# Expert weights in a mixture-of-experts tail: three interleaved runs of blocks, and gathers by row whose indices can be out of bounds

## The reference

```
    padded = (counts + MOE_BLOCK - 1) // MOE_BLOCK * MOE_BLOCK
    ...
    def expert_block(args):
        rows, e = args
        xb = t_pad[rows]
        hid = jax.nn.silu(xb @ w_gate[e]) * (xb @ w_up[e])
        return hid @ w_down[e]
    ...
    y = jnp.zeros((N + 1, D), jnp.float32).at[row_tok].add(y_rows)[:N]
```

## Time and profile before

| | before |
|---|---|
| median of 3 runs | 3672.84 us (3671.2 to 3678.9) |
| the profiled execution | 3669.79 us |
| its span in the trace | 3667.9 us |
| mean granted TensorE clock | 0.981 |
| PE busy, share of the span | 94% |
| DMA issues of expert weights | 48 of 3072.0 KB, 11.8 us to landing (median) |

### The profile page before, as it was taken

One profiled execution on the slowest core, in us unless ns is written; L12 is line 12 of the kernel. 1 busy time (PEld: TensorE's weight loads), 2 busy tenths in 40 slices (PEclk: granted clock), 3 DMA queues, 4 the chain that ended last, 5 costly groups with the idle time before them and its releaser, 6 DMA issues. The chain is left out here.

```text
span 3667.9 us, 32753 instructions
## 1 busy us (share of the span) xinstructions
PE 3460.3 (94%) x11181; PEld 1792.6 (49%) x11181; DVE 1707.4 (47%) x4073; ACT 1046.7 (29%) x2551; POOL 1000.7 (27%) x1395
## 2 busy tenths in 40 slices
PE   4999899999999999999999998899999986999998
PEld 3754355555444644444444444555664433444443
DVE  4656633343355484326655556644454553222222
ACT  3122122221110362002234446643332221222221
POOL 0277767500000393000000002655651001222221
PEclk8999999999999999999999999999999998999999
DMA  3133444433245112222221000000102215999997
GB/s 140 57 131 138 145 157 155 140 126 109 97 160 176 64 36 81 107 88 92 81 85 35 23 9 12 1 1 1 69 25 104 98 75 214 325 336 337 330 331 237
DMA packets 115562, 451.55 MB, mean 123 GB/s; under 512 B 15635, under 2 KB 43155, under 8 KB 103356
## 3 DMA queue, kind: packets, MB, share of 16 engines
q1 hardware_dynamic: 91484, 370.18, 28.3%
q0 software_dynamic: 18432, 58.74, 6.0%
q10 hardware_dynamic: 5472, 20.45, 1.5%
HBM read 340.28 MB, written 117.42 MB: 125 GB/s over the span
## 5 line engine op out<-in xcount | busy, mean ns | idle before, releaser
L142 PE MATMUL pst<-arena 128*128 128x512 f32 (+4 forms) x6554 | 2694.8, 568 | 48.5 <-DMA arena<-in_w_exp 25.5
L142 PEld LDWEIGHTS pst<-arena 128*128 128x128 f32 x6554 | 1243.9, 196 | 1337.6 <-issue 1232.4
L164 POOL TENSOR_TENSOR arena<-arena 128x4 f32<-128x4 f32 (+7 forms) x784 | 403.3, 514 | 455.7 <-DVE arena L2060 395.3
L164 DVE TENSOR_TENSOR arena<-arena 128x1 f32<-128x1 f32 (+8 forms) x1260 | 460.1, 366 | 95.0 <-ACT arena L2290 20.1
L147 PE MATMUL pst<-arena 128*128 128x128 f32 x2161 | 328.1, 286 | 100.3 <-DVE arena L246 52.5
L147 PEld LDWEIGHTS pst<-arena 128*128 128x128 f32 x2161 | 260.7, 146 | 278.5 <-issue 153.2
L1286 POOL TENSOR_SCALAR arena<-arena 128x384 f32<-128x384 f32 (+1 forms) x128 | 151.7, 1213 | 555.8 <-DVE arena L1278 554.6
L153 ACT ACTIVATE arena<-pst,arena 128x128 f32<-128x128 f32 (+1 forms) x630 | 244.8, 485 | 92.7 <-PE pst L147 90.2
L2237 POOL TENSOR_SCALAR arena<-arena 128x512 f32<-128x512 f32 (+3 forms) x160 | 218.6, 1390 | 150.5 <-DVE arena L164 137.2
L167 DVE TENSOR_SCALAR arena<-arena 128x1 f32<-128x1 f32 (+11 forms) x581 | 141.2, 243 | 194.9 <-DMA arena<-in_bc 80.0
L152 ACT ACTIVATE arena<-pst 128x512 f32<-128x512 f32 (+4 forms) x250 | 124.7, 518 | 323.9 <-PE pst L142 197.1
(11 more groups left out here) (200 smaller groups left out, 2070.4 us busy)
## 6 DMA issues: line engine op xcount, KB each, us to landing
arena<-in_w_exp SPq DMA_DIRECT2D x48, 3072.0 KB, 11.8
arena<-in_w_ada SPq DMA_DIRECT2D x48, 512.0 KB, 4.8
rotd<-arena POOLq DMA_DIRECT2D x32, 512.0 KB, 4.0
arena<-rotd SPq DMA_DIRECT2D x32, 512.0 KB, 4.7
arena<-sgd SPq DMA_DIRECT2D x16, 1024.0 KB, 7.1
arena<-pwd SPq DMA_DIRECT2D x32, 416.0 KB, 5.6
pwd<-arena SPq DMA_DIRECT2D x16, 576.0 KB, 6.1
h2d<-arena SPq DMA_DIRECT2D x17, 512.0 KB, 2.9
```

Source lines behind the costliest of these rows:

```text
L142: x = t.do.matmul(o, l, r, start=(i == 0), stop=(i == len(pairs) - 1))
L164: own(v, s).tensor_tensor(o, a, b, op).then_inc(*inc(s, *event))
```

## The change

The order of blocks changes. Program block b no longer stands for place b of the sorted list but for place `sB[b]`: 0, 16, 32, 1, 17, 33, 2, 18, 34 and so on to 15, 31, 47 (48 to 62 stay). So weights slot b % 3 sees one third of the sorted list in order. For program blocks 0 to 47 the experts then are 0 15 22, 1 16 23, 2 17 24, 3 18 25, 4 18 25, 5 18 26, 5 19 26, 6 19 27, 7 19 28, 8 20 28, 9 20 29, 10 21 29, 11 21 30, 12 22 30, 13 22 31, 14 22 31.

The weights of the first three blocks come through SP in two transfers each (`w_up`, 16 KB in each partition, and `w_down`, 8 KB). All later ones come through POOL as gathers by row, again in two parts. The index of partition p is 128 times the expert plus p; where the expert is that of the block three before, 65536 p is added, which puts every row but partition 0's out of bounds, and such rows are not fetched (`oob_is_err=False`). The `up` part waits for `up` of three blocks before, the `down` part for `down` of three blocks before. The row gather is issued one block earlier than it was. The index table `wI` takes a few more operations on DVE, POOL and PE.

```
@@ te_rt, ve_rt
-            trs(t, [(bank(6)[0:1, 0:128], bcol[:, 1:2])]).then_inc(*inc("rt_pe", "bE"))
+            t.do.matmul(bank(6)[:, 0:64], ones, dg, start=True, stop=True).then_inc(*inc("rt_pe", "bE"))
...
-            ts(v, q, bcol[:, 1:2], bcol[:, 1:2], 31.0, None, MIN, BYP, "owner")
+            ts(v, q, bcol[:, 1:2], bcol[:, 1:2], 31.0, None, MIN, BYP)
+            ts(v, q, dg, sB, bcol[:, 2:3], bcol[:, 1:2], ALU.is_equal, MUL, "owner")
             own(v, q).tensor_copy(nbI, pen[:, 31:32]).then_inc(*inc(q, "nb"))
             v.wait_ge(*at("rt_pe", "bE"))
             v.do.tensor_copy(bE[0:1, :], bank(6)[0:1, 0:64]).then_inc(*inc(q, "bE"))
+            ts(v, q, wf, bank(6)[:, 0:64], 128.0, bcol[:, 2:3], MUL, ADD)
+            tt(v, q, same[:, 3:64], wf[:, 3:64], wf[:, 0:61], ALU.is_equal)
+            stt(v, q, same[:, 3:64], same[:, 3:64], bcol[:, 3:4], wf[:, 3:64], MUL, ADD)
+            own(v, q).tensor_copy(wI[:, 3:64], same[:, 3:64]).then_inc(*inc(q, "wI"))
...
@@ the loads
-        def sp_moe_load(s, b):
+        def sp_moe_first(s):
             for i in range(2):
                 s.wait_ge(*at(f"st_out{i}", "x3", NT - 2 + i))
             s.wait_ge(*at("rt_ve", "bE"))
-            s.wait_ge(*at("moe_pe", "down", b - 3, 1))
-            e = s.do.value_load(bE[0:1, b:b + 1], min_val=0, max_val=31)
-            s.do.dma_start(WX[b % 3], T["w_exp"][bass.ds(e, 1), :, :].rearrange("a p n -> p (a n)")
-                           ).then_inc(*dma(f"moe_wx{b % 3}", "wx", b))
+            for b in range(3):
+                e = s.do.value_load(bE[0:1, b:b + 1], min_val=0, max_val=31)
+                s.do.dma_start(WX[b][:, 0:4096], T["w_up"][bass.ds(e, 1), :, :].rearrange("a p n -> p (a n)")
+                               ).then_inc(*dma(f"moe_wf{b}", "up", b))
+                s.do.dma_start(WX[b][:, 4096:6144], T["w_down"][bass.ds(e, 1), :, :].rearrange("a p n -> p (a n)")
+                               ).then_inc(*dma(f"moe_wf{b}", "down", b))
+
+        def po_moe_load(p, b, part):
+            p.wait_ge(*at("rt_ve", "wI"))
+            for i in range(3):
+                p.wait_ge(*at(f"moe_wf{i}", "down", i))
+            if part == "up":
+                p.wait_ge(*at("moe_pe", "up", b - 3))
+                o, w = WX[b % 3][:, 0:4096], T["w_up"]
+            else:
+                p.wait_ge(*at("moe_pe", "down", b - 3, 1))
+                o, w = WX[b % 3][:, 4096:6144], T["w_down"]
+            p.do.indirect_dma_start(out=o, out_offset=None, in_=w.rearrange("a p n -> (a p) n"),
+                                    in_offset=bass.IndirectOffsetOnAxis(ap=wI[:, b:b + 1], axis=0),
+                                    bounds_check=4095, oob_is_err=False
+                                    ).then_inc(*dma(f"moe_{part}{b % 3}", "w", b))
...
@@ POOL's run
-            for b in range(lo, min(lo + 2, hi)):
+            for b in range(lo, min(lo + 3, hi)):
+                if b >= 3:
+                    po_moe_load(p, b, "up")
+                    po_moe_load(p, b, "down")
                 po_moe_gather(p, b)
             for b in range(lo, hi + 1):
-                if b + 2 < hi:
-                    po_moe_gather(p, b + 2)
+                if b + 3 < hi:
+                    po_moe_gather(p, b + 3)
+                    po_moe_load(p, b + 3, "up")
                 if b > lo:
+                    if lo + 3 <= b + 2 < hi:
+                        po_moe_load(p, b + 2, "down")
                     po_moe_scatter(p, b - 1)
```

More of the change, by code:

```diff
@@ L2662, in build @@
         idf = reg(115.5, 64)
+        sB, wf, same, dg = (reg(115.75 + 0.25 * i, 64) for i in range(4))
+        wI = reg(116.75, 64).bitcast(U32)
         bE = reg(117, 64).bitcast(I32)
@@ L2683, in po_rt @@
                       ).then_inc(*inc("rt_po"))
+            p.do.iota(bcol[:, 2:3], [[0, 1]], base=0, channel_multiplier=1, allow_small_or_imprecise_dtypes=True
+                      ).then_inc(*inc("rt_po"))
+            p.do.iota(bcol[:, 3:4], [[0, 1]], base=0, channel_multiplier=65536, allow_small_or_imprecise_dtypes=True
+                      ).then_inc(*inc("rt_po"))
+            p.do.iota(sB[:, 0:48].rearrange("p (a b) -> p a b", a=16), [[1, 16], [16, 3]], base=0, channel_multiplier=0,
+                      allow_small_or_imprecise_dtypes=True).then_inc(*inc("rt_po"))
+            p.do.iota(sB[:, 48:64], [[1, 16]], base=48, channel_multiplier=0, allow_small_or_imprecise_dtypes=True
+                      ).then_inc(*inc("rt_po"))
             p.do.memset(LT, 0.0).then_inc(*inc("rt_po", "made"))
@@ L2811, in ve_rt @@
                 kk = slice(16 * k, 16 * k + 16)
-                tt(v, q, big[:, kk, :], bc(blk[:, k, :], 2, [128, 16, 64]), bc(io128[:, 0:64], 1, [128, 16, 64]),
+                tt(v, q, big[:, kk, :], bc(blk[:, k, :], 2, [128, 16, 64]), bc(sB, 1, [128, 16, 64]),
                    ALU.is_equal)
@@ L2841, in sp_moe_load, with weights_in @@
             s.wait_ge(*at("rt_ve", "bE"))
-            s.wait_ge(*at("moe_pe", "down", b - 3, 1))
-            e = s.do.value_load(bE[0:1, b:b + 1], min_val=0, max_val=31)
-            s.do.dma_start(WX[b % 3], T["w_exp"][bass.ds(e, 1), :, :].rearrange("a p n -> p (a n)")
-                           ).then_inc(*dma(f"moe_wx{b % 3}", "wx", b))
+            for b in range(3):
[18 more added lines that the diff above has]
+                                    ).then_inc(*dma(f"moe_{part}{b % 3}", "w", b))
+        def weights_in(e, b, part):
+            if b < 3:
+                e.wait_ge(*at(f"moe_wf{b}", "down", b))
+            else:
+                e.wait_ge(*at(f"moe_{part}{b % 3}", "w", b))
         def po_moe_gather(p, b):
@@ L2873, in te_moe_up @@
             w3 = WX[b % 3][:, 0:4096].rearrange("p (k n) -> p k n", k=8)
-            t.wait_ge(*at(f"moe_wx{b % 3}", "wx", b))
+            weights_in(t, b, "up")
             t.wait_ge(*at("moe_ac", "xT", b, 1))
@@ L2901, in te_moe_down @@
             w3 = WX[b % 3][:, 4096:6144].rearrange("p (k n) -> p k n", k=2)
+            weights_in(t, b, "down")
             t.wait_ge(*at("moe_ve", "hT", b))
@@ L2930, in y_stored, with po_moe_run @@
                 e.wait_ge(*at(f"moe_ys{b % 2}", "y", b))
-        def sp_moe_run(s, lo, hi):
+        def po_moe_run(p, lo, hi):
             for b in range(lo, min(lo + 3, hi)):
[L2934 to L2938, removed]
-            for b in range(lo, min(lo + 2, hi)):
+                if b >= 3:
+                    po_moe_load(p, b, "up")
+                    po_moe_load(p, b, "down")
                 po_moe_gather(p, b)
             for b in range(lo, hi + 1):
-                if b + 2 < hi:
-                    po_moe_gather(p, b + 2)
+                if b + 3 < hi:
+                    po_moe_gather(p, b + 3)
+                    po_moe_load(p, b + 3, "up")
                 if b > lo:
+                    if lo + 3 <= b + 2 < hi:
+                        po_moe_load(p, b + 2, "down")
                     po_moe_scatter(p, b - 1)
@@ L2991, in sp_fin @@
             y_stored(s, TAILS[0] - 1)
+            for i in range(3):
+                s.wait_ge(*at(f"moe_wf{i}", "down", i))
         def tensor(t):
@@ L3077, in sync @@
             sp_o2(s)
-            guarded(s, sp_moe_run)
+            sp_moe_first(s)
             sp_fin(s)
@@ L3201, in lay @@
     dn = w_down_2[0].reshape(32, 2, 128, 1024).transpose(0, 2, 1, 3).reshape(32, 128, 2048)
-    o["w_exp"] = np.concatenate([gu, dn], 2)
+    o["w_up"], o["w_down"] = gu, dn
     return {k: np.ascontiguousarray(v) for k, v in o.items()}
```

## The result

| | before | after |
|---|---|---|
| median | 3673.64 us (4 runs, 3671.2 to 3678.9) | 3635.15 us (4 runs, 3620.3 to 3638.8) |
| ratio of after to before | | 0.9885, 95% interval 0.9871 to 0.9900 |
| profiled execution, its span | 3669.79, 3667.9 us | 3633.03, 3631.2 us |

The kernel became 1.15% faster. I had forecast 0.9%: the ratio of my numbers, 3640 / 3672.84, is 0.9911 and lies just outside the interval. Applied to 3672.84 us the measured ratio gives 3630.6 us, under the 3634 us that I had called the floor. The place of the gain was right, its size too small and, as the experiments show, its cause mostly another.

The account below looks back on a forecast made before the run. It took transfer time, by a little, as the bound that stalls PE in the expert blocks. Removing 34.3 us of stall and adding 1.4 us of routing took 3672.84 to 3640 us, with an 8-in-10 range of 3634 to 3660.

Parts of the forecast that it names:

- the floor: Whole kernel: PE's pace of 11.40 us a block leaves nothing to gain below 3634 us.
- What bounds the kernel: Expert blocks: PE waits for expert weights, its weight load row 33.6 us; the bound is transfer time, by a little.
- the 11.9 us from the earlier trace: Transfers per expert block: 8.3 us weights plus 3.6 us gather and scatter, more than PE's 11.40 us.
- The stall is 34.3 us: Expert blocks: 45 blocks took 547.3 us against 513.0 without stalls; all 34.3 us should go.
- What is removed: Weights transfers: 15 of 45 blocks skip their fetch, taking 47 MB off 151 MB; mean block 10.1 us, under 11.40.
- The head start: Weights loads: up parts issued 16 us earlier, against at most 11 us behind in ten fetching blocks.
- POOL's issues: Two more issues a block on POOL: four take 6.0 us, inside 11.40 us, so 0 on the path.
- rival C: POOL becomes the bound if issue time goes with bytes of a row: about 3645 us, chance 0.04.
- The routing: Index table operations on DVE and PE before the first gather: +1.4 us, from 0.9 to 1.5 us.
- The sum: Whole kernel: less 34.3, plus 1.4, so median 3672.84 - 32.9 = 3639.9, said as 3640 us.
- The page against: Skill page calling GpSimd loads slower: fetching blocks 12.8 to 14.4 us, a few us of stall left, some 3645 us.

Follow-up runs that it names:

- e2_parts_on_sp: Kernel before with up and down parts loaded apart from SP, each freed and waited for by its own matmuls, nothing skipped: 3636.07 us, ratio 0.9892.
- e3_no_skip: Changed kernel with every weights row fetched, no skips: 3627.19 us, ratio 0.9883 to the kernel before.
- e9_waits_apart: e1_two_tensors with one semaphore for each part, so up and down each wait for their own: 3638.23 us, ratio 0.9925 to the kernel before.
- e1_two_tensors: Kernel before with weights in two tensors, each block loaded by two SP transfers under the same wait: 3751.81 us, ratio 1.0214.
- e11_skip_alone: e6_skip_no_head_start with up waiting for both parts: 3672.07 us, ratio 1.0001 to the kernel before.
- t2_before: Kernel before without an edit, profiled once more: execution 3655.71 us, blocks 570.2 us.
- e6_skip_no_head_start: Changed kernel with the up part's slot freed by down of three blocks before: 3639.52 us, ratio 0.9922 to the kernel before.
- e13_parts_and_early_gather: e2_parts_on_sp reading both parts from one tensor, with POOL's row gather one block earlier: 3620.10 us, ratio 0.9893 to the kernel before.
- e4_all_skipped: Changed kernel with all weights rows but partition 0's skipped for blocks 3 to 47: 3636.05 us, ratio 0.9900 to the kernel before.
- e12_waits_apart_pool: e6_skip_no_head_start without skips, all rows fetched through POOL's queue: 3642.40 us, ratio 0.9937 to the kernel before.
- t1_before: Kernel before without an edit, profiled once more: execution 3674.18 us, blocks 575.1 us.
- e10_before_again: Kernel before without an edit, timed and profiled again: median 3671.10 us, ratio 1.0000, blocks 579.0 us.

## Why the prediction was right in its place and wrong in its size

**What bounds the kernel.** The waits for weights, as read in the earlier trace rows: right, and all of them went. That "the bound is transfer time, by a little", the 11.9 us from the earlier trace rows: wrong. It is the step that failed. The same bytes pass at 350 GB/s in `e2_parts_on_sp` and 348 GB/s in `e3_no_skip` with PE at its floor or within 4 us of it. The bound was the time from issue to landing, 11.8 us, of a load that can be issued only 10.7 us ahead and is waited for whole. `e9_waits_apart` shows it: the same bytes, issued no earlier, took 31 to 41 us less once each part was waited for by itself, where the split alone (`e1_two_tensors`) had cost 73 to 83 us. A DMA share of 0.98 had looked like a full resource. This step had the cause wrong; what put the number outside the range is the next one, and chance.

**The stall is 34.3 us.** Mis-sized. Measured in that one trace it was 34.6; over four traces of before, 573.4 - 534.9 = 38.5 us. I took one execution for the kernel, though the stall has a tail: late loads, behind some of which the clock falls. That is 4.2 us of what I missed.

**What is removed.** 30 of 45 fetch: right by the bytes. That this is what pays: wrong. `e3_no_skip` loses nothing, and `e11_skip_alone` gains nothing on the kernel before. Only without the early slot, in POOL's queue, were the skips worth something (547.6 to 536.7 us).

**The head start** of 16 us I had as cover for ten fetching blocks. With it (`e3_no_skip`) nothing else is needed; but waits apart (`e9_waits_apart`) had most of it without, and I had given them no term at all. The changed kernel has them in `weights_in`, which `te_moe_up` calls with "up" and `te_moe_down` with "down" (after the first three blocks):

```
            if b < 3:
                e.wait_ge(*at(f"moe_wf{b}", "down", b))
            else:
                e.wait_ge(*at(f"moe_{part}{b % 3}", "w", b))
```

I read its two calls as a consequence of the split, and not as the removal of a wait.

**POOL's issues** at nothing: right. Weights gathers took 0.99 us whatever their bytes, less than the 1.06 I used, which ends rival C.

**The routing** +1.4 us: it was +1.8 us to the first `turn`, since a bigger matmul and the operation ahead of it cost 0.67 us and the four behind it 1.12. `up` of block 0 then took 9.84 us instead of 9.46, at a granted clock of 0.68 (3063 to 3073 us) instead of 0.73 (3066 to 3076 us before). Over four traces of each, 42.3 and 44.8 us: +2.5.

**The sum** by its own terms is then -38.5 + 2.5 = -36.0 us, and the four traces of each kernel add -1.9 us upstream (3030.5 and 3028.6), which is chance. That makes -38, beside -38.5 between the medians. The ratio stands for 42.2 us, since one of the four executions after took 3620.3 us, 12.7 us less than the next. It was not traced; the three traces with such low times for their kind (`t2_before`, `e6_skip_no_head_start`, `e13_parts_and_early_gather`) all reached the owners early, at 3017.8 to 3019.5 us. The other three have a mean of 3636.4 us, 38.0 us under the mean of 3674.3 us before. So of the 9.4 us between 3640 and 3630.6 the stall accounts for 4.2, the routing for -1.1, and chance upstream, as far as these traces tell, for some 6. By the -38 of the traces alone the time would have been 3634.8 us, just inside my range and still 5 us under the forecast.

**The floor.** Right for the blocks (`e4_all_skipped`), wrong as a bound of the total: I subtracted a stall that was 4 us too small, and left no room for upstream, which moves by 18 us from run to run.

**The page against.** I had cited the Trainium skill's "DMA: Bandwidth & Descriptors" for slower loads from GpSimd. The 3645 us that I had estimated by it did not come: `e3_no_skip` moved rows of 8 and 16 KB, gather and scatter at 348 GB/s in POOL's queue, and PE never stopped. `e2_parts_on_sp`, with the weights in SP's, moved 350. But both ran at PE's pace, which asks for 4.0 MB in 11.4 us, 350 GB/s, so they don't show which queue is faster. Where the issues came late the runs lean the page's way: 547.6 us with POOL's loads (`e12_waits_apart_pool`), 538.4 with SP's (`e9_waits_apart`), though these two differ in the order of blocks and in the row gather as well.

## What to carry to other kernels

A wait for a whole load is a wait for its last byte. Where two steps read two parts of it, give each its own semaphore before you save bytes; that was worth 31 to 41 us here, and with it and an early slot the skips were worth nothing. A DMA share near 1 doesn't show that the engines are the bound: compare issue to landing with how far ahead the issue can be. And size a stall from several executions: two of four traces here had loads 2 to 4 us late that the first one didn't show.

## What the runs showed of the hardware

- Splitting one 3 MB load into 2 MB and 1 MB under the same wait moved the last landing from 11.8 to 13.3 us after its issue, beside the same gathers and scatters. Row sizes went from 24 KB to 16 and 8 KB with it, so which of the two did it isn't told apart.
- The length of a stall alone didn't tell whether PE's clock fell. Behind waits of 2.08 us (`e11_skip_alone`, granted clock 1.00 from 3100 to 3200 us) and of 3.02 and 3.23 us (`t1_before`, 1.00 in the 15 us around) `up` took 7.1 us; behind waits of 1.88 us (`e10_before_again`), 2.17 us (`e11_skip_alone`) and 2.35 us (`t1_before`) it took 8.8 us, with 0.89 granted in the 15 us around. In `e1_two_tensors` all 20 waits from 3090 to 3640 us, 2.4 to 3.4 us long, had an `up` of 8.5 to 10.2 us behind them. Such a stall costs 1.4 to 2 times its length.
- A gather whose 127 of 128 rows are out of bounds landed 2.6 us (`down`) and 3.1 us (`up`) after its issue in the median (`e4_all_skipped`).
